# FFN input units 5 to 15 with 512-column products, and two weight splits moved at the end of each FFN

## What is computed

```python
def sq_relu_mlp(x, w_in, w_out):
    return jnp.square(jax.nn.relu(x @ w_in)) @ w_out

for i in range(DEPTH):                       # DEPTH = 4
    h = mixer_of_layer_i(x)
    x = layer_norm(alpha * x + h, ln_mix_g[i], ln_mix_b[i])
    x = layer_norm(alpha * x + sq_relu_mlp(x, ffn_w_in[i], ffn_w_out[i]),
                   ln_ffn_g[i], ln_ffn_b[i])
```

## Time and profile before

| | us |
|---|---|
| median of 3 runs | 1495.4 |
| lowest and highest | 1492.81, 1496.49 |
| the profiled execution | 1496.25 |
| its span, first to last instruction | 1494.2 |

### The profile page before, as it was taken

How to read it: one execution, slowest core, us unless ns; L and a number is a source line. 1 busy time by engine, 2 the same in 40 slices (tenths; PEclk the granted TensorE clock), 3 DMA queues, 4 the chain that set the end, 5 groups by cost and what they waited for, 6 DMA issues and landing times. The chain is left out here.

```text
span 1494.2 us, 24380 instructions
## 1 busy us (share of the span) xinstructions
PE 1424.5 (95%) x9643; PEld 1315.2 (88%) x9643; DVE 1007.2 (67%) x1249; ACT 762.3 (51%) x1077; POOL 199.9 (13%) x245
## 2 busy tenths in 40 slices
PE   7899998999999999999999899999998999999996
PEld 7888997999989989999898689998988999899995
DVE  5899899545477575545656466456799899954554
ACT  4776775344434334444355325443477687454441
POOL 2233222532220000000000000000023222200000
PEclk9999999999999999999999899999999999999998
DMA  8666554476666454555544245555656554555550
GB/s 242 200 190 214 170 189 141 148 219 195 216 187 224 156 198 153 202 193 197 187 152 142 85 141 176 198 190 176 196 174 211 184 180 159 170 177 189 186 209 29
DMA packets 198192, 266.96 MB, mean 179 GB/s; under 512 B 11768, under 2 KB 167824, under 8 KB 198080
## 3 DMA queue, kind: packets, MB, share of 16 engines
q1 hardware_dynamic: 188720, 237.72, 48.2%
q0 software_dynamic: 9200, 27.55, 6.0%
q10 hardware_dynamic: 160, 0.13, 0.0%
HBM read 264.19 MB, written 1.18 MB: 178 GB/s over the span
## 5 line engine op out<-in xcount | busy, mean ns | idle before, releaser
L588 PE MATMUL acc<-xT,w_high 128*128 128x256 f32 x3264 | 599.4, 285 | 2.7 <-DVE w_low L1517 2.7
L1517 DVE TENSOR_TENSOR w_low<-raw,w_high 128x2048 fp32r<-128x2048 f32 (+1 forms) x226 | 512.2, 2275 | 98.4 <-ACT w_high L1120 63.6
L1120 ACT ACTIVATE w_high<-raw 128x2048 fp32r<-128x2048 f32 (+1 forms) x226 | 427.2, 1896 | 214.3 <-DMA raw<-in_ffn_w_in 88.9
L588 PEld LDWEIGHTS acc<-xT,w_high 128*128 128x128 f32 x3264 | 515.6, 193 | 7.5 <-issue 3.7
L588 PE MATMUL acc<-xT,w_low 128*128 128x256 f32 x1632 | 463.8, 284 | 0.0
L740 PE MATMUL y<-w_high,opT 128*128 128x512 f32 x1408 | 400.1, 394 | 3.9 <-DVE opT L1940 3.9
L588 PEld LDWEIGHTS acc<-xT,w_low 128*128 128x128 f32 x1632 | 315.2, 193 | 0.0
L740 PEld LDWEIGHTS y<-w_high,opT 128*128 128x128 f32 x1408 | 261.3, 190 | 55.4 <-issue 4.7
L740 PE MATMUL y<-w_low,opT 128*128 128x512 f32 x704 | 224.3, 393 | 0.0
L1536 DVE TENSOR_TENSOR opT<-conv,opT 128x512 fp32r<-128x512 f32 x56 | 39.2, 700 | 263.5 <-issue 236.7
L609 PE MATMUL acc<-w_high,xT 128*128 128x256 f32 (+1 forms) x928 | 181.3, 297 | 10.5 <-DVE xT L1581 9.5
(11 more groups left out here) (206 smaller groups left out, 1181.0 us busy)
## 6 DMA issues: line engine op xcount, KB each, us to landing
raw<-in_ffn_w_in SPq DMA_DIRECT2D x128, 512.0 KB, 4.7
raw<-in_ffn_w_out SPq DMA_DIRECT2D x128, 512.0 KB, 4.5
raw<-in_ssd_w_in SPq DMA_DIRECT2D x96, 512.0 KB, 5.2
E<-cumsum_dram POOLq DMA_DIRECT2D x32, 512.0 KB, 6.1
raw<-in_ssd_w_out SPq DMA_DIRECT2D x32, 512.0 KB, 4.4
raw<-in_sc_w_in SPq DMA_DIRECT2D x24, 512.0 KB, 4.9
raw<-in_na_w_qkv SPq DMA_DIRECT2D x24, 512.0 KB, 4.6
raw<-in_sc_w_out SPq DMA_DIRECT2D x8, 512.0 KB, 4.3
```

Source lines behind the costliest of these rows:

```text
L588: mm = nc.tensor.matmul(bank[:, c * SEQ:(c + 1) * SEQ][:, span], w[:, col:col + P], xT[:, k, low, span], start=(k == 0 and part == 0), sto ...
L1120: nc.scalar.activation(w_high[:, u % SPLIT, c0:k * c], raw[:, u % RAW, c0:k * c], ACT.Copy).then_inc(w_high_done, 1)
L1517: V.tensor_tensor(w_low[:, u % SPLIT, c0:k * c], raw[:, u % RAW, c0:k * c], f(w_high[:, u % SPLIT, c0:k * c]), ALU.subtract).then_inc(w_lo ...
```

## The change

For input units 5 to 15 of each FFN (44 of 64), `features_wide` multiplies `w_high` with both halves of x at once, 512 columns (high beside low), and `w_low` with the high half only, 256 columns. Of a slice k there are two products instead of three; of a unit 32 instead of 48, with the same number of columns in all (12288). Block c = 0 goes into a whole bank `acc`, c = 1 into a whole bank `inner`, alternating between the two of each kind. The partial sum of w_high x low then stands in columns 256 to 511 apart from the rest. ACT copies this part of both banks into `conv` (two copies of 128x256 instead of one relu of 128x512); DVE adds the other part of both (two sums of 128x256) and then takes max(v, 0) * v in one instruction (128x512) instead of the square. Bias windows 5 to 15 of POOL wait for DVE's sums (`mlp_summed`) instead of the relu. At unit 15 the lists of ACT and DVE now go on to the split of u + 4 (fo 14), ahead of the operands that are still to be written.

```diff
+WIDE_FROM = 5
+WIDE = FFN // COLS - WIDE_FROM
...
-                        pool.wait_ge(relu_done, h + 1)
+                        if h < WIDE_FROM:
+                            pool.wait_ge(relu_done, h + 1)
+                        else:
+                            pool.wait_ge(mlp_summed, h - WIDE_FROM + 1)
...
+            def features_wide(u, layer, b):
+
+                wh, wl = weights(u)
+                summed = (mlp_summed, WIDE * layer + b - WIDE_FROM + 1)
+                a, i = (acc_count[0] + b - WIDE_FROM) % 2, (inn_count[0] + b - WIDE_FROM) % 2
+                wide_of[u] = (A[a], I[i])
+                for c, key in enumerate((("a", a), ("i", i))):
+                    take(key, summed)
+                    bank = wide_of[u][c]
+                    for k in range(KT):
+                        col = k * COLS + c * P
+                        nc.tensor.matmul(bank[:, :], wh[:, col:col + P], xT[:, k, :, :].rearrange("p a b -> p (a b)"),
+                                         start=(k == 0), stop=False)
+                        mm = nc.tensor.matmul(bank[:, 0:SEQ], wl[:, col:col + P], xT[:, k, 0, :],
+                                              start=False, stop=(k == KT - 1))
+                used(mm)
...
-                        project(names[("fi", b)], range(NT))
+                        if b < WIDE_FROM:
+                            project(names[("fi", b)], range(NT))
+                        else:
+                            features_wide(names[("fi", b)], s // 2, b)
...
-                            nc.scalar.activation(conv[:, o % 2, :, :], views(bank[:, :]), ACT.Relu).then_inc(relu_done, 1)
+                            else:
+                                result(names[("fi", b)])
                                 act.wait_ge(op_low, o - 1)
+                                for c in range(2):
+                                    ins = nc.scalar.activation(conv[:, o % 2, c, :], wide_of[names[("fi", b)]][c][:, SEQ:2 * SEQ], ACT.Copy)
+                                ins.then_inc(mlp_part, 1)
                         if b >= 1:
-                            split_to(names[("fi", min(b + 1, blocks - 1))] + 2)
+                            split_to(names[("fi", b + 1)] + 2 if b + 1 < blocks else names[("fi", blocks - 1)] + 4)
...
+                            dve.wait_ge(mlp_part, WIDE * (s // 2) + b - WIDE_FROM + 1)
+                            for c in range(2):
+                                y = conv[:, o % 2, c, :]
+                                ins = V.tensor_tensor(y, y, wide_of[u][c][:, 0:SEQ], ALU.add)
+                            ins.then_inc(mlp_summed, 1)
+                            dve.wait_ge(mlp_summed, WIDE * (s // 2) + b - WIDE_FROM + 1)
+                            V.scalar_tensor_tensor(out=conv[:, o % 2, :, :], in0=conv[:, o % 2, :, :], scalar=0.0,
+                                                   in1=conv[:, o % 2, :, :], op0=ALU.max, op1=ALU.mult).then_inc(square_done, 1)
                         if b + 1 < FFN // COLS:
                             split_to(names[("fi", b + 1)] + 2)
+                        else:
+                            split_to(u + 4)
```

More of the change, by code:

```diff
@@ L328, in build @@
         extra = [names[("fi", HEAD_UNITS - 1) if kind == "ffn" else ("z", 1)] for kind, _, names in subs if kind in ("ffn", "ssd")]
-        acc_of = {u: A[k % 2] for k, u in enumerate(u for u in in_units if u not in extra)}
+        wide = [u for u in in_units if units[u][0] == "fi" and units[u][2] >= WIDE_FROM]
+        wide_of = {}
+        acc_of = {u: A[k % 2] for k, u in enumerate(u for u in in_units if u not in extra and u not in wide)}
         acc_of.update({u: Y[0][0] for u in extra})
@@ L1124, in finished @@
                 act.wait_ge(w_used, u + 1)
-                return acc_of[u]
+                return acc_of.get(u)
             def result(u):
@@ L1158, in _ @@
                             o = n["op"] + b
-                            bank = result(names[("fi", b)])
-                            if o >= 2:
+                            if b < WIDE_FROM:
+                                bank = result(names[("fi", b)])
+                                if o >= 2:
+                                    act.wait_ge(op_low, o - 1)
+                                nc.scalar.activation(conv[:, o % 2, :, :], views(bank[:, :]), ACT.Relu).then_inc(relu_done, 1)
+                            else:
+                                result(names[("fi", b)])
                                 act.wait_ge(op_low, o - 1)
-                            nc.scalar.activation(conv[:, o % 2, :, :], views(bank[:, :]), ACT.Relu).then_inc(relu_done, 1)
+                                for c in range(2):
+                                    ins = nc.scalar.activation(conv[:, o % 2, c, :], wide_of[names[("fi", b)]][c][:, SEQ:2 * SEQ], ACT.Copy)
+                                ins.then_inc(mlp_part, 1)
                         if b >= 1:
-                            split_to(names[("fi", min(b + 1, blocks - 1))] + 2)
+                            split_to(names[("fi", b + 1)] + 2 if b + 1 < blocks else names[("fi", blocks - 1)] + 4)
                             m = n["mlp"]
@@ L1595, in _ @@
                         n["mlp"] += 1
-                        result(names[("fi", b)])
-                        dve.wait_ge(relu_done, m + 1)
-                        V.tensor_tensor(conv[:, o % 2, :, :], conv[:, o % 2, :, :], conv[:, o % 2, :, :],
-                                        ALU.mult).then_inc(square_done, 1)
+                        u = names[("fi", b)]
+                        result(u)
+                        if b < WIDE_FROM:
+                            dve.wait_ge(relu_done, WIDE_FROM * (s // 2) + b + 1)
+                            V.tensor_tensor(conv[:, o % 2, :, :], conv[:, o % 2, :, :], conv[:, o % 2, :, :],
+                                            ALU.mult).then_inc(square_done, 1)
+                        else:
[7 more added lines that the diff above has]
+                                                   in1=conv[:, o % 2, :, :], op0=ALU.max, op1=ALU.mult).then_inc(square_done, 1)
                         if b + 1 < FFN // COLS:
                             split_to(names[("fi", b + 1)] + 2)
+                        else:
+                            split_to(u + 4)
                         if 1 <= b <= HEAD_UNITS:
```

5 lines of the change are left out of this document (3 added, 2 removed).

## The result

The changed kernel takes **1500.4 us** in the median of 22 runs (1494.6 to 1508.7), the kernel before 1494.8 in 22 runs beside them (1489.4 to 1498.0). The ratio is 1.0043 with a 95% interval of 1.0031 to 1.0056: slower, by some 6 us, where 3 us less were forecast. The profiled execution is one of the slower ones (1506.85 us).

What follows compares the result with a forecast made beforehand. PE was taken to bound the kernel, with the circle of weights nearly as slow behind it. Layers 0 to 3 at +1.4, -0.5, -1.9 and -2.0 us sum to -3.0, giving 1492.4 us; eight-in-ten range 1487.5 to 1498.

Steps and rivals of the forecast that it cites:

- the moved splits: FFN ends: split of fo 14 ahead of the last operands; FFNs end only 0.6, 0.5, 1.9 and 2.0 us earlier.
- the windows: Layer 0: later bias windows stretch input-unit loads by 0.25 us each, making the split of fo 11 2.0 us later.
- PE's term: Input units from 5 on: fewer products make each unit 5.56 us instead of 5.75, 8.8 us over 44 units.
- the circle: Weight path behind PE: load, ACT's split, operand parts, DVE's split; 10.74 us a turn, 11.0 in layer 0 after.
- reserve: Output units: weights come ahead of PE's need, a margin growing 0.28 us per period instead of 0.48 and staying positive.
- (b): PE's input units: the pair stays near 0.36 us, PE saves next to nothing, 1495 us; chance 0.16.
- the chain: FFN end: from the split of fo 11 through the load and split of fo 14 to the norm, 18.4 us.
- (c): Weight loads and splits in all four FFNs: they fall behind PE, which waits for each output unit, 1501 us; chance 0.14.
- (a): PE's input units: pair runs below 0.348 us, the whole of PE's gain or more arrives, 1488 us; chance 0.12.
- (d): Wide bank in PSUM: not free in time, so the change doesn't do what it says; chance 0.03 with the rest.

Runs made afterwards that it cites:

- e3: The changed kernel with late windows and moved splits both undone, only the wide products left: 1492.1 us, ratio 0.9986 to the kernel before.
- e7: e3 with DVE splitting the next output unit ahead of the operand's low part from unit 4 on: 1489.25 us, ratio 0.9974 to the kernel before.
- e6: e3 with each half's products grouped, eight of 512 columns and then eight of 256: 1491.09 us, ratio 0.9984 to the kernel before.
- e2: The changed kernel with the split of fo 14 back behind the operands, windows still late: 1495.24 us, ratio 1.0005 to the kernel before.
- e1: The changed kernel with bias windows 5 to 15 early again, waiting for ACT's copies, splits still moved: 1498.05 us, ratio 1.0022 to the kernel before.
- e4: The kernel before with all 16 bias windows waiting for DVE's square instead of ACT's relu: 1494.29 us, ratio 0.9999.

## Why the prediction was wrong

**The sum as forecast and as measured.** The forecast of -3.0 us is PE's 8.8, less 3.8 for the moved splits (the four FFNs end 0.6, 0.5, 1.9 and 2.0 us earlier, 5.0 in all and not 8.8), less 2.0 for the windows. The experiments have 2.4 in place of the 8.8 (e3), and 8.3 in place of the 5.8 for the two edits: +5.9, where 5.6 was measured. The largest error is PE's term, by 6.4 us: 4.0 since the pair was taken too short, and 2.4 since only half of the remaining 4.8 arrives once the circle has no reserve (e3 against e7). With 4.8 for PE and the rest as forecast the sum would have been +1.0. The edits make up the other 2.5.

**PE's part: mechanism right, size too large.** The fixed time per product is there, some 12 ns of it (in e6 0.226 us for 512 columns and 0.119 for 256: 256 columns cost 0.107, and 0.012 is left). The step that failed was "both widths and a change between them stand in the rows": the earlier trace rows show one change of width, and at 32 changes in a unit each pair takes 0.353 us, where the grouped order of e6 needs 5.56 / 16 = 0.347. The unit takes 5.64 us and not 5.56, worth 4.8 us in 44 units and not 8.8; 2.4 of these were measured in e3 and 4.9 in e7. The Trainium skill, page "TensorE: Matmul & The Clock Gate", section "Back-to-back issue gap", has 2.5 ns on top of an isolated warm product, and says that in a stream of weight loads and products both set the spacing. The trace does not agree with 2.5 ns for this stream, where e6 shows some 12. Rival (b), which put the time where that figure would have it, had the pair near 0.36 and a gain of at most 1 us; the pair of 0.353 lies between it and the forecast's 0.348.

**The circle and the windows: right in place, nearly right in size.** 0.25 us per load was taken in layer 0; the turn is 11.04 where 11.0 was forecast, and it does not go through the sums. The split of fo 11 came 3.9 us later after the shift of 0.6 us with which the layer began, not 2.0: eight slower loads gave 2.1, and the other 1.8 came in one turn, the third, in which the load of fi 8 took 7.1 us (5.3 before). The kernel before had such loads as well (7.1 us for fi 6) and made them good at nearly 0.5 us per period. That is the missing term: **reserve was counted as margin in the usual case, and not as what absorbs unusual loads.**

**The moved splits: the chain right, its two premises not.** The chain of 18.4 us is right: it is 18.4 in layer 1. But the forecast for the end of each FFN held "if the split of fo 11 comes when it did". Against the norm that begins the FFN it came 3.9 us later in layer 0 (2.0 taken), 1.5 later in layer 2 and 0.4 later in layer 3 (0 taken, or earlier). And the load in the chain was taken at 4.96 us, from a load that had hardly a window beside it. In layer 0 windows ran beside it and it took 7.3; in layer 2, without windows, it took 6.2 (1025.51 to 1031.68 us), and PE waited 0.6 there. In layer 0 the distance from the end of the split of fo 11 to the norm became 442.00 - 419.39 = 22.6 us. By the prediction's sum the chain with the longer load would have ended after 18.4 + 2.4 = 20.8; PE, at half clock after its wait, took 1.9 more, since 0.9 of its 2.7 us fell into time in which it would have waited for the split of fo 14.

Layer by layer, +1.4, -0.5, -1.9 and -2.0 were forecast, and the profiles show +7.5, -0.9, +1.0 and +0.2. In layer 0 the 6.1 us between are 1.9 for the later split, 2.4 for the load and 1.9 for the clock, to within 0.1. In layer 2 the 2.9 us are 1.5 and 1.2, to within 0.2. Layer 1 agrees by luck: the granted clock was 0.85 from 554 to 562 us before and 1.00 in the same stretch of the layer after. In layer 3 the chain does not set the end, and PE's own gain there is 1.2 us at most, not 2.0; what hides it is the stretch ahead of fi 5, where no code changed.

What the edit costs is seen against the wide kernel without it: there the distance is 17.5 us in layer 1 and 18.2 in layer 0 (e3), since PE arrives earlier against the circle, so that a chain of 18.4 us keeps PE waiting. The two edits were priced one by one, and the largest single loss of the profiled execution is where they meet.

**The rivals.** (c), the circle behind PE, gave 1501 and had a chance of 0.14; its time is the one that came, and in good part by luck. It is right that the circle keeps PE waiting, but it asked for a circle longer than PE's period turn after turn, in all four FFNs. Loads of input units took 5.5 us, over the 5.4 it named, in layer 0 only, and even there the turn of 11.04 us is not longer than PE's 11.11. The waits are single ones: in layers 1 and 2 one each at the end (0.6 us) and one each in the middle (0.7 and 0.8), in layer 3 none. (a) failed at its premise, (d) did not happen. The rows that were asked for beforehand told this: the pair at 0.353, operand 14 behind a split that waits for its load, PE waiting for it; only its 1 to 2 us were 3.6 in layer 0 and 0.6 in layer 1.

**The range.** 1498 as the upper end would have held e3 and e2 and missed the whole change by 2.4 us. It took in the costs of windows and splits added up, and not what they cost once the reserve is used up.

**What stays open.** The second SSD stage, 4 us longer in three profiles, goes with a long wait of ACT, but no experiment shows the cause. And of e1's cost of 6.0 us over e3 the ends of the FFNs account for part, by 0.9 us in layer 1 and the waits in its trace; how much is late loads that no reserve absorbs can't be read from one profiled execution. Nor do medians and profiles divide the loss alike: by the medians the late windows cost 2.3 to 3.1 us, in the profiled executions the FFN of layer 0 is 7 to 8 us longer with them.

## What to carry to other kernels

Before an engine that sets the pace is made faster, work out the turn of the next circle behind it (load, splits, operand) with its slowest loads and not its median, since the difference to the pace is what pays for every late transfer, and edits that were free before begin to cost when it is gone. A cost read from a single change of width is not yet the cost of 32 of them in a unit. Price an edit against the kernel as it will be with the other edits in it, and compare a chain with what it competes with there, not with the distance in the old trace. Here the cure was one line that took an operation with a wait out of the circle; it was worth nothing before the change and 9 us after it.

## What the runs showed of the hardware that was not expected

- Alternating products of 512 and 256 columns, each with its own stationary operand, take 0.353 us per pair; grouped, eight and eight, they take 0.226 + 0.119 = 0.345, and 5.56 / 16 = 0.347 with the changes between groups.
- After a wait of 3.6 us PE ran at half clock from 432 to 438 us, and the 31 products after the wait cost 2.7 us more. In e2 the same came after a wait of 3.0 us (granted clock 0.51 from 384 to 387 us), but not after one of 2.2 (1.00 from 434 to 440 us). After waits of 0.8 to 1.3 us in the FFN of layer 0 of the changed kernel the clock stayed at 1.00:

```profile
308.00:312.00 4.00, 4.00 (x19) 3.31 (x18) 1.74 (x1) 0.00 (x0) 0.00 (x0) 1.00 1.00 326
331.00:335.00 4.00, 4.00 (x19) 3.31 (x18) 2.73 (x2) 0.68 (x3) 3.00 (x5) 1.00 1.07 280
```

- Four small transfers of 33 KB beside the load of a unit stretch it by more than their bytes, an eighth of the unit's, would suggest. In e4, which changes only when they go out, the halves of output units took 6.4 us in layer 0 against 4.8 in the kernel before. In the changed kernel the loads of the last three output units of layer 0 took 7.3 to 7.7 us from issue to the landing of both halves, against 4.9 in the median of layer 1, where there are no small transfers.
